# The first expert's weights and the second's gate weights loaded ahead of the last residual store

## The chip, the cores and the metric

The kernel runs on one core of a Trainium2 chip. The metric is the time of one execution on the device in microseconds. Five engines run side by side and meet through semaphores: TensorE (PE, products and transposes through the array), VectorE (DVE), ScalarE (ACT), GpSimd (POOL) and SyncE (SP), which here issues transfers. GpSimd issues transfers too. All of them are carried out by the core's 16 DMA engines.

## The reference, cut to what matters

One layer of a decoder: a token mixer (mLSTM and retention heads), then a mixture of 64 experts. There are 512 prompt tokens and 64 sample tokens, 576 in all, and D_MODEL is 1024. The change lies at the seam between the two halves:

```python
def block(x, c, pos, state, lp):
    ...
    ym, new_state = mixer(hm, pos, state, w_in, b_gates, conv_w, conv_b, m_gn, r_gn, w_out)
    x = x + gt1 * rms_norm(ym, g_mix_post)
    hf = rms_norm(x, g_ffn_pre) * (1.0 + sc2) + sh2
    B, L, D = hf.shape
    yf = moe(hf.reshape(B * L, D), w_router, b_router, w_exp_gate, w_exp_up, w_exp_down,
             w_sh_gate, w_sh_up, w_sh_down).reshape(B, L, D)
    x = x + gt2 * rms_norm(yf, g_ffn_post)

def moe(h, w_router, b_router, we_g, we_u, we_d, ws_g, ws_u, ws_d):
    s = jax.nn.sigmoid(jnp.dot(h, w_router).astype(jnp.float32))
    ...  # group-limited choice of 8 experts for each token, weights wts
    def step(acc, blk):
        e, tok, wt = blk
        xb = h[tok]
        hb = jax.nn.silu(xb @ we_g[e]) * (xb @ we_u[e])
        return acc.at[tok].add(wt[:, None] * (hb @ we_d[e]).astype(jnp.float32)), None
    ...
    shared = (jax.nn.silu(h @ ws_g) * (h @ ws_u)) @ ws_d
```

Each routed expert has gate, up and down weights of 1 MiB each (1024 x 256 in float32); the shared expert has the same sizes.

## The kernel before, in words

The tokens are cut into five tiles of 128 rows (the last has 64). Each engine has one program, whose order is the order of the code; a step waits on semaphores named in the array `S`.

**The seam.** The output product of the mixer (L1260, and L1255 for the last tile) raises `y_mm` once for each tile. ACT and VectorE normalise the rows, add them to the residual stream `x_sb` (L2049, raises `x1_done`) and make the input `hrow2` of the experts (L2060, raises `h2_ready`). For each tile SyncE stores the residual rows to HBM (`mixed_rows`, raises `st_x`) and GpSimd the rows `h` (`ffn_in_rows`, L764, raises `h2_st0` or `h2_st1`). TensorE transposes the `h` rows (`h2T_t`), makes the router's logits (L1433, L1442) and, whenever it has nothing else, steps of the shared expert's gate and up products (L1477, 64 steps, of which the trace shows two records each), spread by hand between the other operations.

**The routing.** VectorE first clears and fills small tables (L2064 to L2074). Ahead of these it waits for `ld_br` to reach 32, which stands for two loads: the router's bias (L590) and the shared expert's down weights `dn_s` (L468). Then it waits for `rl_sig`, ACT's sigmoid of the logits (L1027, L1028), chooses experts (L2086 to L2111, raises `msk_ready`), waits for the ranks of the tokens within each expert, which TensorE sums (`positions`, L1487 and L1489), and makes the first one-hot tables (`place`, L2189, raises `P_ready`). With these TensorE finds the tokens of a block (`find_idx`, L1520), VectorE writes their indices, GpSimd gathers their rows (L774), TensorE transposes them (L1533), and the expert loop begins.

**The expert loop.** Each block of 128 token slots has an up product (L1545), a transpose of the hidden rows (L1556) and a down product (L1568). The weights lie in four slots, and SyncE's one queue loads them: slots 0, 1 and 3 in `mem`, slot 2 in `x_sb`. The first three experts are fixed, all others come in the order of a sorted table (`ptab`), which raises `tab_ready`. Slot 0 and the gate half of slot 1 overlap the mixer's output weights `wo` in `mem`, which are read until the last `y_mm`; the rest of slot 1 overlaps `hrow2`; slot 2 overlaps the residual rows and needs `st_x`. GpSimd clears its gather buffers in between (L766 after `h2T_t`, L768 after `st_x`).

**SyncE's order around the change.** It stores the five residual tiles (L593), each after its `x1_done`; loads `dn_s`; waits for `h2T_t` and both `h2_st`; loads gate, up and down weights of experts 0 and 1, and gate and up of expert 2; waits for `tab_ready`; loads expert 3 and what is missing of expert 2.

Of the kernel before, what the change touches and what calls it, by code (L numbers as in the profile page):

```python
# [14 lines left out]
P = 128  # L15
D = 1024
KC = D // P
# [5 lines left out]
NT = NCH + 1  # L23
ROWS = [P] * NCH + [NS]
NCOND = 1 + NB
H = 4
# [9 lines left out]
FE = 256  # L36
# [69 lines left out]
def carve(region, at, shape, rows=P, dt=F32):  # L106

    n = 1
    for s in shape:
        n *= s  # L110
    if dt != F32:
        n //= 2
    v = region[0:rows, at:at + n]
    if dt != F32:
        v = v.bitcast(dt)
    if len(shape) == 2:
        v = v.rearrange("p (a b) -> p a b", a=shape[0])
    elif len(shape) == 3:
        v = v.rearrange("p (a b c) -> p a b c", a=shape[0], b=shape[1])
    return v, at + n  # L120
# [6 lines left out]
def build(nc, A, O, K):  # L127

    ctx = ExitStack()
    with ctx:  # L130
        def sb(name, shape, dt=F32):
            return ctx.enter_context(nc.sbuf_tensor(name, shape, dt))

        def sem(name):
            return ctx.enter_context(nc.semaphore(name))
# [4 lines left out]
        x1_d = nc.dram_tensor("mixed_rows", [T, D], F32, kind="Internal").ap()  # L140
# [3 lines left out]
        x_sb = sb("x_sb", [P, NT, D])  # L144
# [22 lines left out]
        grows, _ = carve(aux, 0, [len(GRN), T], H)  # L167
# [95 lines left out]
        adaA, _ = carve(mem, at, [2, 512])  # L263
# [18 lines left out]
        WSZ = 3 * KC * FE  # L282
# [8 lines left out]
        W_AT = [0, WSZ, None, w2_at]  # L291
# [8 lines left out]
        xg3, _ = carve(x_flat, 2 * KC * FE, [D])  # L300
# [11 lines left out]
        dn_s, at = carve(mem, at, [FJ, D])  # L312
# [44 lines left out]
        S = {n: sem(n) for n in names}  # L357
# [24 lines left out]
        for bi, (nm, _) in enumerate(BLOCKS):  # L382
            if nm in ("mv", "rv"):
                UNITS += [("tok", nm, bi, t) for t in range(NT)]
            else:
                UNITS += [("chan", nm, bi, c) for c in range(4)]
            if nm == "mv":
                UNITS += [("gate", "g", bi, 0)]
# [57 lines left out]
        def slot(r):  # L446

            return r % WSLOTS if r < NE else OVSLOTS[(r - NE) % len(OVSLOTS)]
# [5 lines left out]
        def wview(r):  # L454

            if slot(r) == XSLOT:
                return x_flat[:, 0:2 * KC * FE].rearrange("p (m c f) -> p m c f", m=2, c=KC), dnX
            w = mem[:, W_AT[slot(r)]:W_AT[slot(r)] + WSZ]
            gu = w[:, 0:2 * KC * FE].rearrange("p (m c f) -> p m c f", m=2, c=KC)
            dn = w[:, 2 * KC * FE:WSZ].rearrange("p (j d) -> p j d", j=FJ)  # L460
            return gu, dn

        def load_up(sp, w, src, s):

            sp.dma_start(w, src.rearrange("(p c) f -> p c f", c=KC)).then_inc(s, 16)

        def load_down(sp, dn, d, s):
            sp.dma_start(dn, d.rearrange("(j p) d -> p j d", p=P)).then_inc(s, 16)  # L468

        def one_expert(name, e):  # L470
            return A[name][0, bass.ds(e, 1)].rearrange("a d f -> (a d) f")
# [36 lines left out]
        def _(sp):  # L508
# [79 lines left out]
            load_up(sp, gu_s[:, 1, :, :], A["w_sh_up"][0], S["ld_ws"])  # L588
            sp.wait_ge(S["st_out"], 16 * NST)
            sp.dma_start(brow, A["b_router"][0].partition_broadcast(P)).then_inc(S["ld_br"], 16)  # L590
            for t in range(NT):
                sp.wait_ge(S["x1_done"], t + 1)
                sp.dma_start(x1_d[t * P:t * P + ROWS[t], :], x_sb[0:ROWS[t], t, :]).then_inc(S["st_x"], 16)  # L593
            load_down(sp, dn_s, A["w_sh_down"][0], S["ld_br"])
            sp.wait_ge(S["h2T_t"], NT)
            sp.wait_ge(S["h2_st0"], 16 * ((NT + 1) // 2))
            sp.wait_ge(S["h2_st1"], 16 * (NT // 2))

            def load_gate_up(r, e):
                gu, _ = wview(r)  # L600
                load_up(sp, gu[:, 0, :, :], one_expert("w_exp_gate", e), S[f"ld_gu{slot(r)}"])
                load_up(sp, gu[:, 1, :, :], one_expert("w_exp_up", e), S[f"ld_gu{slot(r)}"])

            def load_dn(r, e):
                _, dn = wview(r)
                sp.dma_start(dn, one_expert("w_exp_down", e).rearrange("(p j) d -> p j d", j=FJ)).then_inc(S[f"ld_d{slot(r)}"], 16)

            for r in range(2):
                load_gate_up(r, r)
                load_dn(r, r)  # L610
            sp.wait_ge(S["st_x"], 16 * NT)
            load_gate_up(XSLOT, XSLOT)
            sp.wait_ge(S["tab_ready"], 1)
            ids = {}
            id3 = sp.value_load(ptab[0:1, NPRE:NPRE + 1], min_val=0, max_val=NE - 1)
            load_gate_up(NPRE, id3)
            sp.wait_ge(S["gu_mm"], NSH)
            load_dn(XSLOT, XSLOT)
# [210 lines left out]
        def _(act):  # L829
# [249 lines left out]
            for i, (t, _) in enumerate(COMBINE):  # L1079
                n = ROWS[t]  # L1080
                if i < LAST:
                    act.wait_ge(S["yl_sum"], i + 1)
                    step(a(yjunk[0:n], yo[0:n, i % 2, :], ACT.Square, accum_out=stat[0:n, 10, t:t + 1]))
                    a(stat[0:n, 11, t:t + 1], stat[0:n, 10, t:t + 1], ACT.Sqrt, bias=epsc[0:n, :], scale=1.0 / D).then_inc(S["yf_rt"], 1)
                else:
                    act.wait_ge(S["yd_sum"], NT + 1)
                    step(a(yjunk[0:n, 0:512], yo[0:n, i % 2, 0:512], ACT.Square, accum_out=stat[0:n, 10, t:t + 1]))
                    step(a(stat[0:n, 13, t:t + 1], stat[0:n, 10, t:t + 1], ACT.Identity, bias=epsc[0:n, :], scale=1.0 / D))
                    act.wait_ge(S["yl_sum"], i + 1)
                    step(a(yjunk[0:n, 512:D], yo[0:n, i % 2, 512:D], ACT.Square, accum_out=stat[0:n, 0, t:t + 1]))  # L1090
                    a(stat[0:n, 11, t:t + 1], stat[0:n, 0, t:t + 1], ACT.Sqrt, bias=stat[0:n, 13, t:t + 1], scale=1.0 / D).then_inc(S["yf_rt"], 1)
# [3 lines left out]
        def _(pe):  # L1095
# [107 lines left out]
            def key_rows(h):  # L1203
                _, k = QK(h)
                for c in range(NCH):
                    tr(ps[2][:, c * P:(c + 1) * P], k[:, c * P:(c + 1) * P], ident[:, :])
# [1239 lines left out]
```

## Time and profile before

| | us |
|---|---|
| median of three timed runs | 1137.02 |
| lowest and highest | 1135.15, 1137.31 |
| span of the profiled execution | 1136.7 |
| TensorE busy in it | 1096.6 |
| VectorE, ScalarE, GpSimd busy | 462.9, 236.6, 137.3 |

The profiled execution is the same program taken by the hardware profiler; its span runs from the first to the last instruction. Operations are shown with their start and duration. A timeline merges equal operations that follow each other (x8), with the start of the first and the time until the last one ends. In square brackets stands how long the engine was idle before, and what released it. Products overlap in the array and their ends are modelled, so neighbours can overlap by some tenths of a microsecond. A stretch of the view by windows gives the busy time of each engine, the granted TensorE clock as a fraction of 2.4 GHz, the mean busy share of the DMA engines and what they moved.

### The profile page before, as it was taken

The page shows a single profiled execution, that of the slowest core. Times are in us where ns is not written, and L with a number is a line of the kernel's source. Part 1 is how long each engine was busy: PE and PEld are TensorE (multiplying, and loading weights), DVE is VectorE, ACT ScalarE, POOL GpSimd, SP SyncE. Part 2 cuts the span into 40 slices and gives each one's busy share as a digit, 9 for nine tenths or more (in the row PEclk, how much of TensorE's full clock was granted, in tenths as well). Part 3 has the DMA queues.
Part 4 walks back from the last instruction along what each step waited for, and adds up shares of the span by engine and source line. Part 5 has one row for each costly group of instructions (what it writes and reads, how often), then busy time and mean ns, then how long its engine had stood idle before and what let it go on. Part 6 is the DMA issues. An engine that isn't in the chain of part 4 may idle for free.

```text
span 1136.7 us, 16992 instructions
## 1 busy us (share of the span) xinstructions
PE 1096.6 (96%) x6443; PEld 576.4 (51%) x6443; DVE 462.9 (41%) x1286; ACT 236.6 (21%) x516; POOL 137.3 (12%) x163
## 2 busy tenths in 40 slices
PE   6999999999999999999989999999999999999896
PEld 3456677777877545754433443443343444343232
DVE  2218541665456645842264223223233232231157
ACT  4131241222233123111101111111111111111111
POOL 0110000000020110121111112111112111121100
PEclk9999999999999999999999999999999999999999
DMA  9978742042270372899999999999999999999898
GB/s 317 308 262 297 227 79 54 21 84 56 65 260 2 138 267 82 343 354 340 414 414 400 421 406 421 419 403 385 417 409 353 418 408 385 415 398 363 311 406 342
DMA packets 80743, 337.17 MB, mean 297 GB/s; under 512 B 10756, under 2 KB 27496, under 8 KB 52366
## 3 DMA queue, kind: packets, MB, share of 16 engines
q1 hardware_dynamic: 62606, 287.32, 66.4%
q0 software_dynamic: 18048, 48.68, 11.7%
q8 instruction: 54, 0.88, 0.3%
q14 instruction: 35, 0.29, 0.1%
HBM read 311.30 MB, written 37.24 MB: 307 GB/s over the span
## 4 chain that ended last, share of the span: by engine, by line
PE 87%; DMA 8%; DVE 2%; ACT 1%; issue 1%; SPq 1%; DVEq 0%; POOLq 0%; ACTq 0%
PE bank L1545 27%; PE bank L1568 15%; PE bank L1241 10%; PE bank L1260 5%; DMA mem<-in_w_exp_down 4%; PE bank L1533 3%; DMA mem<-expert_out_rows 3%; PE bank L1359 3%; PE bank L1360 3%; PE bank L1154 3%; PE bank L1477 3%; PE bank L1238 3%; PE bank L1129 1%; PE bank L1556 1%; PE bank L1324 1%
## 5 line engine op out<-in xcount | busy, mean ns | idle before, releaser
L1545 PE MATMUL bank<-mem 128*32 128x512 f32 (+2 forms) x1424 | 304.5, 594 | 2.6 <-issue 1.6
L1545 PEld LDWEIGHTS bank<-mem 128*32 128x32 f32 (+2 forms) x1424 | 100.2, 126 | 159.3 <-issue 157.9
L1568 PE MATMUL bank<-mem 128*32 128x512 f32 (+2 forms) x712 | 158.6, 599 | 5.1 <-DMA mem<-in_w_exp_down 5.1
L2231 DVE COPY mem<-bank 128x512 f32<-128x512 f32 x48 | 33.2, 692 | 292.2 <-PE bank L1533 292.2
L1545 PE MATMUL bank<-x_sb,mem 128*32 128x512 f32 (+2 forms) x480 | 141.6, 594 | 1.1 <-issue 1.1
L1241 PE MATMUL bank<-hT,mem 128*128 128x288 f32 x512 | 133.3, 409 | 1.0 <-ACT mem L919 1.0
L1241 PEld LDWEIGHTS bank<-hT,mem 128*128 128x128 f32 x512 | 93.8, 190 | 25.8 <-issue 2.4
L1049 ACT ACTIVATE mem<-bank 128x256 f32<-128x256 f32 x48 | 18.5, 385 | 316.7 <-PE bank L1556 316.5
L1568 PEld LDWEIGHTS bank<-mem 128*32 128x32 f32 (+2 forms) x712 | 49.1, 126 | 63.8 <-issue 60.3
L1568 PE MATMUL bank<-hT,mem 128*32 128x512 f32 (+2 forms) x240 | 72.8, 596 | 1.1 <-ACT mem L1049 1.1
L1545 PEld LDWEIGHTS bank<-x_sb,mem 128*32 128x32 f32 (+2 forms) x480 | 43.6, 127 | 59.1 <-issue 59.1
L2246 DVE COPY hT<-bank 128x512 f32<-128x512 f32 x48 | 33.2, 692 | 86.4 <-PE bank L1568 86.3
L774 POOL DMA_INDIRECT mem<-ffn_in_rows,idxg x32 | 33.2, 1036 | 269.8 <-DVE idxs L2227 214.4
L790 POOL DMA_INDIRECT expert_out_rows<-hT,idxs x48 | 48.8, 1017 | 115.8 <-DVE hT L2246 108.6
L1055 ACT ACTIVATE hT<-bank 128x512 f32<-128x512 f32 x48 | 28.7, 597 | 147.7 <-PE bank L1568 147.7
L1260 PE MATMUL bank<-mem 128*128 128x512 f32 x128 | 56.3, 594 | 0.0
L2189 DVE SCALAR_TENSOR_TENSOR mem<-mem,c_full 128x160 bf16<-128x160 f32 (+3 forms) x77 | 43.9, 571 | 0.3 <-issue 0.3
L1359 PE MATMUL bank<-hT,mem 128*128 128x288 f32 x128 | 42.3, 412 | 0.0
L1360 PE MATMUL bank<-hT,mem 128*128 128x288 f32 x128 | 41.5, 406 | 0.0
L1260 PEld LDWEIGHTS bank<-mem 128*128 128x128 f32 x128 | 23.8, 190 | 27.4 <-issue 27.3
L2239 DVE SCALAR_TENSOR_TENSOR mem<-mem,wtab,bank 128x128 f32<-128x128 f32 x96 | 29.4, 347 | 18.5 <-ACT mem L1043 18.5
L1037 ACT ACTIVATE mem<-bank 128x512 f32<-128x512 f32 x48 | 28.7, 598 | 39.2 <-PE bank L1533 39.2
(403 smaller groups left out, 1290.4 us busy)
## 6 DMA issues: line engine op xcount, KB each, us to landing
mem<-in_w_exp_gate SPq DMA_DIRECT2D x48, 1024.0 KB
mem<-in_w_exp_up SPq DMA_DIRECT2D x48, 1024.0 KB
mem<-in_w_exp_down SPq DMA_DIRECT2D x48, 1024.0 KB
mem<-in_w_ada SPq DMA_DIRECT2D x8, 2048.0 KB, 9.8
x_sb<-in_w_exp_gate SPq DMA_DIRECT2D x16, 1024.0 KB
x_sb<-in_w_exp_up SPq DMA_DIRECT2D x16, 1024.0 KB
hT<-in_w_exp_down SPq DMA_DIRECT2D x16, 1024.0 KB
mem<-in_w_in SPq DMA_DIRECT2D x7, 2048.0 KB, 14.2
```

Of the source, the lines that this page charges most:

```text
L790: pool.indirect_dma_start(y_d[:, :], bass.IndirectOffsetOnAxis(idxs[:, q:q + 1], 0), yo[:, q % 2, :], None, bounds_check=T * TOPK - 1, oob ...
L1154: i = mm(ps[t][:, :], hT[:, k, t * P:(t + 1) * P], ring[:, 0, k * 512:(k + 1) * 512], start=k == 0, stop=k == KC - 1)
L1238: i = mm(bank[0:n, 0:2 * DH], hT[:, k, c * P:c * P + n], w[:, k, 2 * DH * hf:2 * DH * (hf + 1)], start=k == 0, stop=k == KC - 1)
L1241: i = mm(bank[:, 0:TH], w[:, k, c * P:(c + 1) * P], hT[:, k, hf * TH:(hf + 1) * TH], start=k == 0, stop=k == KC - 1)
L1260: i = mm(y_half(t, hf), yT(k)[:, t * P:t * P + n], wo[:, k, hf * 512:(hf + 1) * 512], start=k == 0, stop=k == 2 * H - 1)
L1359: mm(A0[:, 0:TH], st, hT[:, k, 0:TH], start=k == 0, stop=k == KC - 1)
L1360: i = mm(A1[:, 0:TH], st, hT[:, k, TH:T], start=k == 0, stop=k == KC - 1)
L1477: i = mm(ps[bu if m else bg][:, 0:TH], gu_s[:, m, k, j * P:(j + 1) * P], hT[:, k, hf * TH:(hf + 1) * TH], start=k == 0, stop=k == KC - 1)
L1533: i = tr(ps[c // 4][:, (c % 4) * BLK:(c % 4 + 1) * BLK], xg[g][:, c * P:(c + 1) * P], ident[:, :])
L1545: i = mm(bank[sl, :].rearrange("p (m f) -> p m f", m=2), xT[:, j % 2, c * BLK + sl.start:c * BLK + sl.stop], wview(r)[0][:, :, c, :], star ...
L1568: i = mm(ps[4 + hf][sl, :], hhT[:, k * BLK + sl.start:k * BLK + sl.stop], wview(r)[1][:, k, hf * 512:(hf + 1) * 512], start=k == 0, stop=k ...
L2189: return stt(pm, p.to_broadcast([P, NT, w]), off, iota[:, 0:w].unsqueeze(1).to_broadcast([P, NT, w]), ALU.add, ALU.is_equal)
```

## The change

Only SyncE's program changes. After the first four residual stores it waits for the fifth `y_mm`, asks for gate, up and down weights of expert 0, then makes the fifth residual store, then asks for the gate weights of expert 1 and for `dn_s`. After the waits for `h2T_t`, `h2_st0` and `h2_st1` only the up and down weights of expert 1 are left, and expert 2 follows as before. The sizes, the addresses and the semaphores of all transfers stay.

```diff
-            for t in range(NT):
+            def load_gate(r, e):
+                load_up(sp, wview(r)[0][:, 0, :, :], one_expert("w_exp_gate", e), S[f"ld_gu{slot(r)}"])
+            def load_up_half(r, e):
+                load_up(sp, wview(r)[0][:, 1, :, :], one_expert("w_exp_up", e), S[f"ld_gu{slot(r)}"])
+            def load_gate_up(r, e):
+                load_gate(r, e)
+                load_up_half(r, e)
...
+            def x1_store(t):
                 sp.wait_ge(S["x1_done"], t + 1)
                 sp.dma_start(x1_d[t * P:t * P + ROWS[t], :], x_sb[0:ROWS[t], t, :]).then_inc(S["st_x"], 16)
+            for t in range(NT - 1):
+                x1_store(t)
+            sp.wait_ge(S["y_mm"], NT)
+            assert W_AT[0] + WSZ <= W_AT[1] and W_AT[1] + KC * FE <= 2 * H * D
+            load_gate_up(0, 0)
+            load_dn(0, 0)
+            x1_store(NT - 1)
+            load_gate(1, 1)
             load_down(sp, dn_s, A["w_sh_down"][0], S["ld_br"])
             sp.wait_ge(S["h2T_t"], NT)
             sp.wait_ge(S["h2_st0"], 16 * ((NT + 1) // 2))
             sp.wait_ge(S["h2_st1"], 16 * (NT // 2))
...
-            for r in range(2):
-                load_gate_up(r, r)
-                load_dn(r, r)
+            load_up_half(1, 1)
+            load_dn(1, 1)
             sp.wait_ge(S["st_x"], 16 * NT)
             load_gate_up(XSLOT, XSLOT)
```

SyncE's order at the seam before (`mixed_rows` are the residual stores, `in_w_sh_down` is `dn_s`, a name after "waits" is the semaphore):

```order
L593 DMA mixed_rows<-x_sb 128x1024 [waits x1_done] x4
L593 DMA mixed_rows<-x_sb 64x1024 [waits x1_done]
L468 DMA mem<-in_w_sh_down 128x2x1024
L465 DMA mem<-in_w_exp_gate 128x2048 [waits h2_st1,h2_st0,h2T_t]
L465 DMA mem<-in_w_exp_up 128x2048
L606 DMA mem<-in_w_exp_down 128x2048
L465 DMA mem<-in_w_exp_gate 128x2048
L465 DMA mem<-in_w_exp_up 128x2048
L606 DMA mem<-in_w_exp_down 128x2048
L465 DMA x_sb<-in_w_exp_gate 128x2048 [waits st_x]
```

And the same place now, where the line numbers of the later part are shifted by the new code:

```order
L608 DMA mixed_rows<-x_sb 128x1024 [waits x1_done] x4
L465 DMA mem<-in_w_exp_gate 128x2048 [waits y_mm]
L465 DMA mem<-in_w_exp_up 128x2048
L604 DMA mem<-in_w_exp_down 128x2048
L608 DMA mixed_rows<-x_sb 64x1024 [waits x1_done]
L465 DMA mem<-in_w_exp_gate 128x2048
L468 DMA mem<-in_w_sh_down 128x2x1024
L465 DMA mem<-in_w_exp_up 128x2048 [waits h2_st1,h2_st0,h2T_t]
L604 DMA mem<-in_w_exp_down 128x2048
L465 DMA x_sb<-in_w_exp_gate 128x2048 [waits st_x]
```

Three weight loads now stand ahead of the fifth residual store, and a fourth between it and `dn_s`.

On VectorE nothing moves. This is its order at the start of the routing, the same before and now but for the line numbers; `ld_br` is the semaphore of `dn_s` and of the router's bias:

```order
L2060 TENSOR_TENSOR mem<-mem 64x128x8 [waits h2_st0,h2T_t,dch]
L2064 MEMSET aux 128x120 [waits ld_br]
L2065 MEMSET aux 128x120
L2066 MEMSET mem 64x64
L2067 MEMSET mem 64x32
L2068 MEMSET mem 128x32
L2069 MEMSET mem 128x128
L2070 CAST mem<-c_full 128x128
L2071 MEMSET stat 64x1
L2072 TENSOR_SCALAR mem<-mem 128x320
L2073 TENSOR_TENSOR mem<-c_full,mem 128x320
L2074 TENSOR_SCALAR mem<-mem 128x320 [waits dch]
```

The first of these small operations waits for `dn_s`, though none of them reads it.

## Rows read from the trace of the kernel before

**Rows 1.** The page: busy us (share) by engine; shares of the chain.
```profile
PE 1096.6 (96%) x6443; PEld 576.4 (51%) x6443; DVE 462.9 (41%) x1286; ACT 236.6 (21%) x516; POOL 137.3 (12%) x163
...
PE 87%; DMA 8%; DVE 2%; ACT 1%; issue 1%; SPq 1%; DVEq 0%; POOLq 0%; ACTq 0%
```

**Rows 2.** TensorE's waits, whole span: releaser, us in total, times, longest.
```profile
PE bank L1568 <- DMA mem<-in_w_exp_down: 5.1, 3, 2.5
```

**Rows 3.** Timeline of SyncE's queue, 440 to 490: start, us, what.
```profile
444.06 9.00 SPq L593 DMA_DIRECT2D mixed_rows<-x_sb  x2
453.51 0.39 SPq L468 DMA_DIRECT2D mem<-in_w_sh_down  x1
461.23 0.33 SPq L465 DMA_DIRECT2D mem<-in_w_exp_gate  x1
...
485.98 0.35 SPq L465 DMA_DIRECT2D mem<-in_w_exp_gate  x1
```

**Rows 4.** Stretches: busy us by engine (operations), granted clock, DMA share, GB/s.
```profile
453.50:455.50 2.00, 2.00 (x18) 1.12 (x18) 0.95 (x2) 1.95 (x4) 0.00 (x0) 1.00 0.89 176
458.00:458.50 0.50, 0.48 (x7) 0.48 (x8) 0.00 (x0) 0.00 (x0) 0.24 (x1) 1.00 0.05 16
459.00:461.00 2.00, 2.00 (x11) 1.34 (x10) 1.90 (x6) 0.43 (x2) 2.00 (x2) 1.00 0.60 131
462.00:482.00 20.00, 20.00 (x98) 15.22 (x98) 17.66 (x110) 3.25 (x8) 0.11 (x1) 1.00 0.99 403
472.00:480.00 8.00, 8.00 (x42) 6.15 (x41) 7.58 (x25) 0.41 (x1) 0.00 (x0) 1.00 1.01 423
```

**Rows 5.** Timeline of VectorE, 457 to 480; brackets: idle before, releaser.
```profile
458.73 0.16 DVE L2064 MEMSET aux<- 128x120 f32 x1 [0.76 <-DMA mem<-in_w_sh_down]
...
459.42 2.20 DVE L2070 CAST mem<-c_full 128x128 bf16<-128x128 f32 x1
...
462.40 0.24 DVE L2074 TENSOR_SCALAR mem<-mem 128x320 bf16<-128x320 bf16 x1
464.11 0.49 DVE L2086 TENSOR_TENSOR aux<-mem,aux 128x320 f32<-128x320 f32 x1 [1.47 <-ACT mem L1028]
...
472.32 0.18 DVE L2111 TENSOR_SCALAR mem<-aux 64x64 bf16<-64x64 f32 x1
...
476.18 0.33 DVE L2123 CAST mem<-aux 128x320 bf16<-128x320 f32 x1
...
478.71 0.82 DVE L2189 SCALAR_TENSOR_TENSOR mem<-mem,c_full 128x640 bf16<-128x640 f32 x1
```

**Rows 6.** Timeline of TensorE's products, 439 to 490.
```profile
439.97 7.09 PE L1255 MATMUL bank<-mem 128*64 128x512 f32 x32
...
473.17 0.33 PE L1487 MATMUL bank<-mem 128*128 128x384 bf16 x1
...
479.64 0.27 PE L1520 MATMUL bank<-mem 128*128 128x7 bf16 x5
...
488.47 1.96 PE L1545 MATMUL bank<-mem 128*128 128x512 f32 x4
```

**Rows 7.** Waits of TensorE's weight loads, 470 to 490.
```profile
PEld bank L1520 <- DVE mem L2189: 0.2, 1, 0.2
```

**Rows 8.** Timeline of GpSimd, 440 to 490.
```profile
449.34 0.53 POOL L764 DMA_DIRECT2D ffn_in_rows<-mem  x1 [14.96 <-DVE mem L2060]
...
458.81 1.83 POOL L766 MEMSET mem<- 128x2048 f32 x1
460.55 0.98 POOL L768 MEMSET x_sb<- 128x1024 f32 x1
```

**Rows 9.** Stretch behind TensorE's longest stand, columns as in rows 4.
```profile
584.40:587.70 3.30, 3.30 (x5) 1.33 (x4) 3.27 (x2) 0.00 (x0) 0.20 (x1) 0.50 1.02 426
```

**Rows 10.** TensorE's products, 567 to 590: the two longest stands for weights.
```profile
568.92 3.64 PE L1568 MATMUL bank<-mem 128*32 128x512 f32 x32 [1.62 <-DMA mem<-in_w_exp_down]
...
583.48 5.40 PE L1568 MATMUL bank<-mem 128*128 128x512 f32 x8 [2.54 <-DMA mem<-in_w_exp_down]
```

More of the change, by code:

```diff
@@ L590, in _, with load_dn @@
             sp.dma_start(brow, A["b_router"][0].partition_broadcast(P)).then_inc(S["ld_br"], 16)
-            for t in range(NT):
+            def load_gate(r, e):
[5 more added lines that the diff above has]
+                load_up_half(r, e)
+            def load_dn(r, e):
+                _, dn = wview(r)
+                sp.dma_start(dn, one_expert("w_exp_down", e).rearrange("(p j) d -> p j d", j=FJ)).then_inc(S[f"ld_d{slot(r)}"], 16)
+            def x1_store(t):
                 sp.wait_ge(S["x1_done"], t + 1)
                 sp.dma_start(x1_d[t * P:t * P + ROWS[t], :], x_sb[0:ROWS[t], t, :]).then_inc(S["st_x"], 16)
+            for t in range(NT - 1):
[6 more added lines that the diff above has]
+            load_gate(1, 1)
             load_down(sp, dn_s, A["w_sh_down"][0], S["ld_br"])
@@ L597, in _ @@
             sp.wait_ge(S["h2_st1"], 16 * (NT // 2))
[L599 to L606, printed above, removed]
-            for r in range(2):
-                load_gate_up(r, r)
-                load_dn(r, r)
+            load_up_half(1, 1)
+            load_dn(1, 1)
             sp.wait_ge(S["st_x"], 16 * NT)
```

## The prediction

> **What bounds the kernel now.** I read the page first. TensorE is busy 96% of the span and holds 87% of the chain that ended last [rows 1]. So a load that arrives earlier saves time only where TensorE waits for it, and a load that arrives later costs only where TensorE ends up waiting. TensorE's list of waits over the whole span comes next [rows 2]. Expert down weights account for 5.1 us over three waits. The two longest end at 583.48 and 568.92 us [rows 10], over 100 us behind the edit. The first expert's first product (L1545) starts at 488.47 with no wait in front of it [rows 6].
>
> Are those three waits within the change's reach? Only if the transfer queues still owe work from the edit when the expert loop begins. From 461.23 on SyncE issues eight weight loads of 1 MiB, one behind the other [rows 3]. The stretch 462 to 482 moves 403 GB/s x 20 us = 8.06 MB of their 8.39 MB, and the rest needs 0.8 us at the 423 GB/s of 472 to 480 [rows 4]. So they end at about 482.8, while the next weight load is issued at 485.98, when the table of sorted experts is ready [rows 3]. The queue is empty between, and the early start of four loads can't be handed on beyond that point. The gain that the edit could have is therefore near zero: the two products it brings forward are not waited for.
>
> What it can cost lies in the stretch before. VectorE's row of operations there is dense: memsets from 458.73, the routing from 464.11, the first one-hot table of tokens (L2189) at 479.53, and TensorE's list search (L1520) behind it at 479.64 [rows 5, 6]. TensorE's weight loads show a wait of 0.2 us for exactly this L2189 [rows 7]. So the routing on VectorE sets when TensorE passes 479.6, with no slack, though TensorE looks fully busy. Whatever delays the routing delays all that follows by as much.
>
> **The change part by part.** No instruction is added on any compute engine. SyncE gets one wait (for y_mm, the last output product), and the same transfers in another order.
>
> (a) The new wait. It is met when the 32 products of L1255 end, 439.97 + 7.09 = 447.06 [rows 6]. The store queued behind it waits for x1_done of the last tile, which comes at 452.6 (before, that store's issue ends at 453.06) [rows 3]. SyncE stands idle between, so the wait itself costs nothing. Without that cover it would hold back a store by some microseconds, for which only a memset on GpSimd waits.
>
> (b) The shared expert's down weights land later. Before, that load is issued at 453.51 with only a 256 KiB store ahead of it, and VectorE stands 0.76 us in front of L2064 for it, until 458.73 [rows 3, 5]. It waits there for ld_br, the semaphore of this load, though the memsets don't touch the data. In the changed order the same SyncE queue holds, ahead of it and with it, 3 MiB + 256 KiB + 1 MiB + 1 MiB = 5.25 MiB = 5.51 MB, beginning at 447.1. At 423 GB/s [rows 4] that is 13.0 us. From issue to the start of data I take 1.7 us: 8.39 MB need 19.8 us, ended at 482.8, so began at 463.0, and were issued at 461.23. Data run from 448.8 to 461.8. GpSimd's store of 512 KiB of h rows, issued at 449.34 [rows 8], goes through the same engines and adds 0.52 MB / 423 = 1.2 us: 463.1. This is the lower end. The two transfers of 64 rows go slowly in the trace of before: 453.5 to 455.5 moved 352 KB at an engine share of 0.89, 1.0 us more than its bytes need, and 459 to 461 moved 262 KB at a share of 0.60, 1.2 us in all [rows 4]. Both added give 465.3, the upper end. Mixed with large loads they should cost less than alone, so I take 0.9 of the 2.2 us: last data at 464.0. From the end of data (458.0: the next half microsecond moves 16 GB/s [rows 4]) to L2064 it was 0.75 us; so L2064 starts at about 464.75, between 463.85 and 466.05, **6.0 us later** (5.1 to 7.3).
>
> The queue order is the crux of this term, and rows can't show it directly, since no small load stands behind large ones there. The Trainium skill (DMA: Bandwidth & Descriptors, section on queues, rings and completion order) says that each DMA engine consumes one queue's descriptors in ring order, and the section on issuing engines says that GpSimd's transfers interleave with SyncE's on the same engines. By that the down weights can't pass the four expert loads. If they could share alike with them, the landing would be near 458 and the term near zero.
>
> (c) The block of small operations gets shorter. From L2064 to the end of L2074 it took 458.73 to 462.64 = 3.91 us, of which 2.20 us is one cast of 128x128 (L2070), while a cast of 128x320 (L2123) takes 0.33 us [rows 5]. GpSimd's two memsets ran from 458.81 to 461.53, and the cast ended at 461.62 [rows 5, 8]. In the new order they still run then: the first waits for TensorE's transposes, the second for the last residual store, which lands at some 448.8 + 8.0 + 1.2 + 0.8 = 458.8 to 459.8. They are over before 464. So the cast takes 0.3 us and the block 2.0 us: **-1.9 us**. The Trainium skill (SBUF — State Buffer, the part on the two sides of SBUF) says that VectorE and GpSimd share one pair of ports, held for a whole instruction; the trace agrees with it, 2.20 us against 0.33. If the cast were long for a reason of its own, (c) would be zero.
>
> (d) The slack. VectorE then waited 1.47 us for ACT's sigmoid (L1028) before L2086 [rows 5]. ACT's chain (transposes, router, sigmoid) takes no data of these loads, so its time stays: **-1.47 us**.
>
> Sum: 6.0 - 1.9 - 1.47 = **+2.6 us**, between 5.1 - 3.4 = 1.7 and 7.3 - 3.4 = 3.9. L2086 starts at 466.7 in place of 464.11.
>
> (e) What TensorE sees of it. The mask is ready at 472.50 (L2111), TensorE's L1487 starts at 473.17 [rows 5, 6]. Later by 2.6 us: 475.1, so TensorE stands about 2.0 us there. It then works through 12 steps of shared products, and stands another 0.6 us at L1520, until VectorE's table is there at 482.1. Behind L1520 the slots table, the first gather and the sorted ids all hang on VectorE and shift alike; so does the load at 485.98. The whole loop shifts by 2.6 us.
>
> (f) The rest. The second expert's gate weights go before the down weights too (counted in (b)); its up and down weights and the third expert's gate and up weights are issued when the h rows are stored, as before. Those four MiB are through by about 476. They are needed first at 488.5, so they cost nothing; what hides them is TensorE's shared products. If this cover were gone, each MiB would cost 2.5 us. The first gather meets an empty queue either way.
>
> Against the profiled execution: 1136.7 + 2.6 = 1139.3. The median of the timed runs is 1137.02, 0.3 above that span, so I add the sum to the median: **1139.6**.
>
> **The rivals.**
> 1. *The routing is late, as summed*: 1137.02 + 1.7 to 3.9 = 1138.7 to 1140.9. Chance 0.50.
> 2. *The new stand drops TensorE's clock.* After the stand of 2.54 us before 583.48 the granted clock was 0.50 for some 3.4 us, and 8 products of L1568 took 5.40 us, while the group after the other stand took 3.64 [rows 9, 10]. After the stand of 1.62 us before 568.92 its products ran at full pace [rows 10]. The new stand of 2.0 us lies between these two, so it is open. The price is 1.8 us, of which the second stand at L1520 (0.6) takes up its part: +1.2, in all 3.8, so 1140.8 (1139.9 to 1142). Chance 0.20.
> 3. *Nothing is late enough* (not slower). The down weights land by 462.1, so that block (c) ends before ACT's sigmoid: the decisive point is 3.4 us later than before. For it speaks that the packets of four loads might share the engines with the fifth; against it, 5.5 MB need 13 us. 1136.4 to 1138.2, most likely 1137.0. Chance 0.15.
> 4. *Faster.* As in 3, and the stand at 583.48 falls under the length that drops the clock, which saves 1.8 us: 1137.0 - 1.8 = 1135.2. It would decide if the loads in front of it came 1 us earlier relative to TensorE. Against it speaks the queue that runs empty before 485.98. Chance 0.10.
> 5. *The cast keeps its 2.20 us*: 6.0 - 1.47 = 4.5, so 1141.5. Chance 0.05.
>
> **How the numbers follow.** The likeliest case is the first, so the forecast is its 1139.6. A measurement here can tell some 0.2% (2.3 us) from no change, so "slower" begins at 1139.3, close to the forecast. From case 1 about two thirds lie above it (0.33), from 2 nearly all (0.19), from 5 all (0.05): 0.57. Faster is case 4 and little else: 0.10. The rest, 0.33, is within. The range holds cases 1, 2, 5 and most of 3: 1136.8 to 1141.8.
>
> **What would show it.** Right: L2064 on VectorE waits for the down weights until about 464.7; L2070 takes 0.3 us; L2086 starts near 466.7 and no longer waits for ACT; TensorE stands about 2 us before L1487, with VectorE as the releaser, and about 0.6 us before L1520; the first L1545 starts near 491.1. Wrong: a wait for the down weights that ends before 462 (then case 3), a half clock between 474 and 480 (case 2), a long L2070 (case 5), or other waits for expert weights near 569 and 583 (case 4).

## The result, and the profile after

In the rows, line numbers of the changed kernel are 13 above those of before from the seam on (L2064 is L2077, L2086 is L2099, L1487 is L1500, L1520 is L1533, L1545 is L1558; in e3 it is 12). The changed kernel takes 1140.97 us (median of five runs, 1139.8 to 1143.8) against 1137.02 us before (five runs, 1135.15 to 1137.72). The ratio is 1.0044, with an interval from 1.0032 to 1.0055: slower by 3.6 to 6.3 us, with 5.0 us at its centre, while the medians lie 3.95 us apart. A repeat against 15 runs of the kernel before (e7 below) gives 1.0034 and 3.8 us. The forecast was 1139.6, slower by 2.6. The sign and the mechanism hold, the size does not. Among the runs told below, one of e2 (1171.93 us) and two of e4 (1427.82 and 1629.35) ran at a lower granted clock: the medians count them, the ratios don't.

In every run for which both are listed, the time of an execution is 1.8 to 1.9 us above its span. The profiled execution of after has a span of 1142.0 us and was the slowest of the five; by the same 1.8 us the profiled execution of before (1136.7) stands for 1138.5, which is 1.5 above its median. So the 5.3 us between the two profiles are not the measure of the change; what happens at one place in them is.

The page of after, engines and shares of the chain, answers to [rows 1]. TensorE's work is the same; VectorE has gone from 2% to 5% of the chain:

```profile
PE 1100.1 (96%) x6443; PEld 577.7 (51%) x6443; DVE 460.9 (40%) x1286; ACT 236.3 (21%) x516; POOL 137.0 (12%) x163
...
PE 84%; DMA 6%; DVE 5%; ACT 2%; issue 2%; SPq 0%; DVEq 0%; ACTq 0%
```

SyncE's queue, which answers to [rows 3] (start, us, operation). Gate, up and down of the first expert go at 446.71 to 448.6; the last residual store, the second gate and the shared down weights follow from 452.19; the load that waits for the sorted ids is at 489.26 in place of 485.98:

```profile
446.71 0.33 SPq L465 DMA_DIRECT2D mem<-in_w_exp_gate  x1
...
452.19 0.47 SPq L608 DMA_DIRECT2D mixed_rows<-x_sb  x1
...
454.06 0.52 SPq L468 DMA_DIRECT2D mem<-in_w_sh_down  x1
464.23 0.33 SPq L465 DMA_DIRECT2D mem<-in_w_exp_up  x1
...
489.26 0.35 SPq L465 DMA_DIRECT2D mem<-in_w_exp_gate  x1
```

VectorE, which answers to [rows 5] (in brackets the idle time before, and what ended it). The reader is to see three things. The first small operation waits 7.92 us for the shared down weights, where it was 0.76. The cast takes 0.16 us, where it was 2.20. And the first routing operation (467.41) has no bracket: the wait of 1.47 us for ACT is gone.

```profile
465.49 0.16 DVE L2077 MEMSET aux<- 128x120 f32 x1 [7.92 <-DMA mem<-in_w_sh_down]
...
466.18 0.16 DVE L2083 CAST mem<-c_full 128x128 bf16<-128x128 f32 x1
...
467.13 0.24 DVE L2087 TENSOR_SCALAR mem<-mem 128x320 bf16<-128x320 bf16 x1
467.41 0.49 DVE L2099 TENSOR_TENSOR aux<-mem,aux 128x320 f32<-128x320 f32 x1
```

GpSimd's two memsets, which answer to [rows 8], are over at 461.13, four microseconds before VectorE's small operations start:

```profile
458.41 1.83 POOL L779 MEMSET mem<- 128x2048 f32 x1
460.15 0.98 POOL L781 MEMSET x_sb<- 128x1024 f32 x1
```

TensorE, which answers to [rows 6]. It stands 2.90 us for the mask and 0.37 us for the first one-hot table; the first up product starts at 491.73. Its waits from 440 to 500, listed by total, name the same two and put both down to VectorE (the first line is the last output product of the mixer):

```profile
439.58 7.09 PE L1268 MATMUL bank<-mem 128*64 128x512 f32 x32
446.60 4.15 PE L1490 MATMUL bank<-hT,mem 128*128 128x288 f32 x16
...
475.84 0.34 PE L1500 MATMUL bank<-mem 128*128 128x384 bf16 x1 [2.90 <-DVE mem L2124]
...
482.87 0.28 PE L1533 MATMUL bank<-mem 128*128 128x7 bf16 x5 [0.37 <-DVE mem L2202]
...
491.73 7.11 PE L1558 MATMUL bank<-mem 128*128 128x512 f32 x16
```

The two executions run 0.4 us apart at this point, since TensorE's first step of shared products starts here at 446.60 and in the kernel before at 446.98:

```profile
446.98 4.15 PE L1477 MATMUL bank<-hT,mem 128*128 128x288 f32 x16
```

So I measure from this step to the first up product. It is 488.47 - 446.98 = 41.49 us before [rows 6] and 491.73 - 446.60 = 45.13 us after: **+3.64 us**, all of it in the stretch that the prediction named. From the first up product to the end of the span it is 648.2 before and 650.3 after. The experiments tell whether these other 2.1 us belong to the change.

### The profile page after: what moved, and what is told of

Its sections match the earlier page's. It is cut to its first block, busy times and chain, and to the rows that moved or that the text cites. A ratio compares the mean times of both kernels' runs of the same rounds, so it can differ in the third digit from the quotient of the medians.

```text
span 1142.0 us, 16992 instructions
## 1 busy us (share of the span) xinstructions
PE 1100.1 (96%) x6443; PEld 577.7 (51%) x6443; DVE 460.9 (40%) x1286; ACT 236.3 (21%) x516; POOL 137.0 (12%) x163
## 4 chain that ended last, share of the span: by engine, by line
PE 84%; DMA 6%; DVE 5%; ACT 2%; issue 2%; SPq 0%; DVEq 0%; ACTq 0%
PE bank L1558 27%; PE bank L1581 14%; PE bank L1254 10%; PE bank L1273 5%; DMA mem<-in_w_exp_down 4%; PE bank L1546 3%; PE bank L1372 3%; PE bank L1373 3%; PE bank L1167 3%; PE bank L1251 2%; PE bank L1672 1%; PE bank L1142 1%; PE bank L1569 1%; DMA mem<-in_w_sh_down 1%; PE bank L1337 1%
## 5 line engine op out<-in xcount | busy, mean ns | idle before, releaser
L1558 PE MATMUL bank<-mem 128*32 128x512 f32 (+2 forms) x1424 | 306.3, 595 | 2.8 <-issue 1.7
L1558 PEld LDWEIGHTS bank<-mem 128*32 128x32 f32 (+2 forms) x1424 | 101.1, 126 | 159.5 <-issue 158.1
L1558 PE MATMUL bank<-x_sb,mem 128*32 128x512 f32 (+2 forms) x480 | 143.3, 598 | 2.1 <-issue 2.1
L1558 PEld LDWEIGHTS bank<-x_sb,mem 128*32 128x32 f32 (+2 forms) x480 | 43.9, 128 | 61.4 <-issue 61.4
```

The lines of the kernel that those rows point to most:

```text
L1558: i = mm(bank[sl, :].rearrange("p (m f) -> p m f", m=2), xT[:, j % 2, c * BLK + sl.start:c * BLK + sl.stop], wview(r)[0][:, :, c, :], star ...
```

## The experiments

Each is compared with runs of the kernel before on the same chip: e1 to e4 with 31 of them, e5 to e7 with 15 on another chip. The theory: the whole loss is that VectorE waits, ahead of the routing, for a load that now stands behind four MiB in SyncE's queue. The main rival: the early weight loads cost by themselves, because they crowd the stores or disturb the loop.

**e1_own_semaphore: keep the early loads, take away what VectorE waits for.** The shared down weights raise a semaphore of their own (one that has done its earlier work by then), on which only TensorE waits, at the end of the kernel.

```diff
-            load_down(sp, dn_s, A["w_sh_down"][0], S["ld_br"])
+            load_down(sp, dn_s, A["w_sh_down"][0], S["ld_cv"])
...
-                    pe.wait_ge(S["ld_br"], 32)
+                    pe.wait_ge(S["ld_cv"], 32)
...
-            dve.wait_ge(S["ld_br"], 32)
+            dve.wait_ge(S["ld_br"], 16)
```

> The changed order of loads, but the shared expert's down weights raise a semaphore of their own, and VectorE's small operations wait for the router's bias alone. If the whole loss is the wait for those down weights: they land at about 465 as before, the small operations start near 457.6, TensorE has no stand before the ranks' product, the expert loop starts where it did before the change, and the time is 1137.0 (within 1 us). If the early weight loads themselves cost (by crowding the stores of the residual and h rows, or in the loop): 1140 to 1141, as the change.

Measured: 1136.34 us against 1137.09, ratio 0.9994 (0.9984 to 1.0004). The early loads are there: SyncE issues the first at 446.17. VectorE has its small operations behind it long before ACT's sigmoid, which is what it waits for again:

```profile
456.99 0.16 DVE L2077 MEMSET aux<- 128x120 f32 x1
...
457.68 0.23 DVE L2083 CAST mem<-c_full 128x128 bf16<-128x128 f32 x1
...
458.02 1.78 DVE L2085 TENSOR_SCALAR mem<-mem 128x320 bf16<-128x320 bf16 x1
...
463.18 0.49 DVE L2099 TENSOR_TENSOR aux<-mem,aux 128x320 f32<-128x320 f32 x1 [2.35 <-ACT mem L1041]
```

and TensorE has no stand:

```profile
446.06 4.15 PE L1490 MATMUL bank<-hT,mem 128*128 128x288 f32 x16
...
487.54 7.11 PE L1558 MATMUL bank<-mem 128*128 128x512 f32 x16
```

487.54 - 446.06 = 41.48 us, to 0.01 us the value of before. The loss is gone with the early loads in place, so crowding as a cause of the loss falls. Crowding itself is there: SyncE's wait for the stores of the h rows ends at 463.84 in e1, 3.5 us later than before on the same time scale (461.23 - 0.92), and likewise at 464.23 in the change. Here nothing on the path waits for it. Any gain falls too: with the loss taken away, four early MiB are worth nothing that can be measured (the interval leaves room for 1.8 us of gain at most).

**e2_late_down_alone: the late load without the early ones.** The kernel before, with one line moved:

```diff
-            load_down(sp, dn_s, A["w_sh_down"][0], S["ld_br"])
             sp.wait_ge(S["h2T_t"], NT)
             sp.wait_ge(S["h2_st0"], 16 * ((NT + 1) // 2))
             sp.wait_ge(S["h2_st1"], 16 * (NT // 2))
...
+            load_down(sp, dn_s, A["w_sh_down"][0], S["ld_br"])
             for r in range(2):
                 load_gate_up(r, r)
```

> The kernel before with only one edit: the shared expert's down weights are asked for behind the waits for the h rows, right ahead of the first expert's weights. No weight of an expert is loaded early. If the late landing is the whole cause: data run from 462.9 to 465.4, the small operations start at about 466.1, the first routing operation at 468.1 in place of 464.1, the loop 4.0 us later, time 1141.0. If crowding by early expert weights is the cause: 1137.0.

Measured: 1140.82 us against 1137.09, ratio 1.0032 (1.0018 to 1.0046). VectorE and TensorE:

```profile
465.11 0.16 DVE L2064 MEMSET aux<- 128x120 f32 x1 [8.35 <-DMA mem<-in_w_sh_down]
```

```profile
445.77 4.15 PE L1477 MATMUL bank<-hT,mem 128*128 128x288 f32 x16
...
475.47 0.34 PE L1487 MATMUL bank<-mem 128*128 128x384 bf16 x1 [3.35 <-DVE mem L2111]
...
491.36 7.11 PE L1545 MATMUL bank<-mem 128*128 128x512 f32 x16
```

This whole execution runs 1.21 us ahead of the kernel before at that point (445.77 against 446.98), so, moved onto the time scale of the kernel before, the small operations start at 466.3; the forecast was 466.1. The way to the first up product is 45.59 us, +4.10 against a forecast of 4.0. One moved line gives the whole loss without any early expert weight.

**e3_three_ahead: one MiB less.** The second expert's gate weights go back behind the waits:

```diff
             x1_store(NT - 1)
-            load_gate(1, 1)
             load_down(sp, dn_s, A["w_sh_down"][0], S["ld_br"])
...
-            load_up_half(1, 1)
+            load_gate_up(1, 1)
```

> The change without the second expert's early gate weights: 3 MiB in place of 4 ahead of the down weights. By the queue order one MiB is 2.5 us, so the small operations start at 463.0 in place of 465.5, the first routing operation at 464.9, which is 1.2 us late in place of 3.65; time 1138.2. If the loss doesn't follow the bytes ahead of the down weights: 1141.

Measured: 1138.48 us against 1137.09, ratio 1.0014 (1.0004 to 1.0023). VectorE:

```profile
461.44 0.16 DVE L2076 MEMSET aux<- 128x120 f32 x1 [5.17 <-DMA mem<-in_w_sh_down]
...
463.36 0.49 DVE L2098 TENSOR_TENSOR aux<-mem,aux 128x320 f32<-128x320 f32 x1
```

This execution's first shared step starts at 445.27, so the small operations start 461.44 - 445.27 = 16.17 us behind it. With four MiB (after) it is 465.49 - 446.60 = 18.89: one MiB is 2.7 us, near the 2.5 expected. Its way to the first up product is 42.41 us (487.68 - 445.27), +0.92 against the 1.2 expected. In the kernel before the same distance is 458.73 - 446.98 = 11.75, so here they are 4.42 us late. The slack (the shorter cast and the wait for ACT) takes 3.5 us of that; the rest follows the bytes ahead of the load.

**e4_down_first: the same loads, another order.** All four early expert loads are kept in front of the waits, but behind the shared down weights, so they start at 453.67, 7 us later than in the change:

```diff
-            load_gate_up(0, 0)
-            load_dn(0, 0)
             x1_store(NT - 1)
-            load_gate(1, 1)
             load_down(sp, dn_s, A["w_sh_down"][0], S["ld_br"])
+            load_gate_up(0, 0)
+            load_dn(0, 0)
+            load_gate(1, 1)
```

> The same loads as in the change, but in the order last residual store, shared down weights, then the first expert's three and the second's gate weights, all before the waits for the h rows. By the queue order the down weights land at 458.3 and the time is 1137.0. If any expert load in that stretch costs: above 1138.5.

Measured: 1137.1 us against 1137.09, ratio 1.0002 (0.9991 to 1.0012). VectorE:

```profile
458.88 0.16 DVE L2077 MEMSET aux<- 128x120 f32 x1 [1.47 <-DMA mem<-in_w_sh_down]
...
459.58 1.48 DVE L2083 CAST mem<-c_full 128x128 bf16<-128x128 f32 x1
...
463.56 0.49 DVE L2099 TENSOR_TENSOR aux<-mem,aux 128x320 f32<-128x320 f32 x1 [1.47 <-ACT mem L1041]
```

The way to the first up product is 41.48 us again (446.44 to 487.92). It is the order that costs. The loads behind the down weights are not quite without effect: the small operations start 12.44 us behind the first shared step, 0.7 us more than before, although a landing at 458.3, earlier than before, was expected. The cover takes it up.

**e5_before_own_semaphore: the same wait taken from the kernel before.** The three lines of e1, applied to the kernel before.

> The kernel before, with VectorE's wait for the shared expert's down weights taken away in the same manner (they raise a semaphore of their own). The small operations start 0.76 us earlier, but behind them VectorE waits for ACT's sigmoid anyway (1.47 us before, some 2.2 us now), so the time stays 1137.1. If that wait already cost something in the kernel before: 1136.3.

Measured: 1136.64 us against 1136.85, ratio 0.9993 (0.9983 to 1.0003), no change that can be measured. VectorE:

```profile
457.74 0.16 DVE L2064 MEMSET aux<- 128x120 f32 x1
...
458.77 2.67 DVE L2072 TENSOR_SCALAR mem<-mem 128x320 bf16<-128x320 bf16 x1
...
463.93 0.49 DVE L2086 TENSOR_TENSOR aux<-mem,aux 128x320 f32<-128x320 f32 x1 [1.81 <-ACT mem L1028]
```

It starts earlier and waits for ACT longer (1.81 us for 1.47; 2.2 were expected, but now L2072 is long, 2.67 us where it was 0.24), and the way is 41.48 us. So in the kernel before the wait of 0.76 us for the down weights cost nothing; it had 3.4 us of cover in all (1.47 of waiting and the 2 us by which the cast was longer than after the change).

**e6_down_behind_up: a larger dose.** The change, with the shared down weights one load further back, behind the waits for the h rows and the second expert's up weights:

```diff
             load_gate(1, 1)
-            load_down(sp, dn_s, A["w_sh_down"][0], S["ld_br"])
...
             load_up_half(1, 1)
+            load_down(sp, dn_s, A["w_sh_down"][0], S["ld_br"])
             load_dn(1, 1)
```

> The change with the shared down weights one step later still, behind the second expert's up weights, and so behind the waits for the h rows: issued near 464.6, data from 465.7 to 470.7, small operations at 471.4, first routing operation at 473.3 in place of 463.7. If TensorE follows VectorE one for one: loop 9.6 us late, time 1146.7. If the loop can take up some of it (its waits for weights of 5 us in all are shorter then, since the weights come early relative to TensorE): down to 1143.

Measured: 1146.38 us against 1136.85, ratio 1.0081 (1.0066 to 1.0097), that is +9.5 by the medians. VectorE and TensorE:

```profile
472.43 0.16 DVE L2077 MEMSET aux<- 128x120 f32 x1 [13.39 <-DMA mem<-in_w_sh_down]
...
474.35 0.49 DVE L2099 TENSOR_TENSOR aux<-mem,aux 128x320 f32<-128x320 f32 x1
```

```profile
482.78 0.50 PE L1500 MATMUL bank<-mem 128*128 128x384 bf16 x1 [8.39 <-DVE mem L2124]
...
483.89 8.40 PE L1490 MATMUL bank<-hT,mem 128*128 128x288 f32 x24
...
500.96 7.11 PE L1558 MATMUL bank<-mem 128*128 128x512 f32 x16
```

The first routing operation comes 474.35 - 448.05 = 26.30 us behind the first shared step, where it was 17.13 (464.11 - 446.98), so 9.2 us late (9.6 were expected, counted from 463.7 in place of the 464.11 of [rows 5]; the time forecast was 1146.7). None of it comes back in the loop, which takes 647.6 us from the first up product to the end, within the scatter of the table below. In this one execution, which was the slowest of its four (1150.48, the others 1146.1 to 1146.5), the way to the first up product is even 11.4 us longer. The stand of 8.39 us begins at 474.39. In its middle, at 478.5, TensorE's granted clock falls to 0.50, and it stays there for 10 us (a stretch with busy us by engine, granted clock, DMA share and GB/s):

```profile
478.50:488.50 10.00, 5.72 (x16) 4.08 (x17) 9.44 (x48) 0.00 (x0) 0.00 (x0) 0.50 0.04 17
```

24 records of shared products take 8.40 us there, where they take 6.07 in the profile of after. Whether the other three runs had this half clock no profile shows; their mean granted clocks, 0.989, 0.989 and 0.991, are not above the 0.991 of this one.

**e7_change_again: the change once more.**

> The change itself once more, for its spread and a second profile. The expert loop starts 3.65 us late again and the median is 1140.7 to 1141.0. Whether the half-clock stretches lie elsewhere (a second one cost 1.7 us in the first profile, near 1061) tells whether what lies beyond 3.65 us belongs to the change: if it does, the loop of this profile is again longer than before by about 2 us; if it is scatter, it is not.

Measured: 1140.62 us against 1136.85, ratio 1.0034 (1.0021 to 1.0048). VectorE and TensorE:

```profile
466.42 0.16 DVE L2077 MEMSET aux<- 128x120 f32 x1 [8.06 <-DMA mem<-in_w_sh_down]
```

```profile
447.37 4.15 PE L1490 MATMUL bank<-hT,mem 128*128 128x288 f32 x16
...
476.77 0.34 PE L1500 MATMUL bank<-mem 128*128 128x384 bf16 x1 [3.06 <-DVE mem L2124]
...
492.67 7.11 PE L1558 MATMUL bank<-mem 128*128 128x512 f32 x16
```

The way to the first up product is 45.30 us, +3.81; behind it the rest of the span is 1138.8 - 492.67 = 646.1 us, 2.1 *shorter* than before, where the first profile of the change was 2.1 longer. All in one table, from the rows above and each execution's span:

| kernel | MiB of expert weights ahead of the shared down weights | first shared step to first up product, us | from there to the end, us | time against before, us |
|---|---|---|---|---|
| before | 0 | 41.49 | 648.2 | |
| e4, down weights first | 0 | 41.48 | 646.7 | 0.0 |
| e5, before without the wait | wait gone | 41.48 | 648.9 | -0.2 |
| e1, change without the wait | wait gone | 41.48 | 648.7 | -0.8 |
| e3 | 3 | 42.41 | 649.0 | +1.4 |
| the change | 4 | 45.13 | 650.3 | +3.95 |
| the change again | 4 | 45.30 | 646.1 | +3.8 |
| e2, late without early loads | 0, but issued late | 45.59 | 647.8 | +3.7 |
| e6 | 5, and issued late | 52.91 | 647.6 | +9.5 |

The fourth column goes up and down by 4 us with no relation to the third. The 2.1 us by which it is longer in the first profile of the change do not come back in the second, so they are scatter between executions; what makes it, these profiles do not settle.

## Why the prediction was right and where it was wrong

**The bound, and no gain: right.** TensorE was named as the bound with no wait for the first expert's weights, and the queue as empty before the sorted ids. After the change the eight loads are through by 476 (476 to 478 moves 16 GB/s), the next one is issued at 489.26, and e1 and e4 show that early loads alone give nothing.

**(a) The new wait costs nothing: right.** The 32 products of the last output tile end at 439.58 + 7.09 = 446.67, the first weight load goes at 446.71, and the store behind the wait still goes at 452.19, which is 452.57 on the time scale of before, where its issue ended at 453.06 [rows 3].

**(b) The landing of the shared down weights: the right mechanism, too small a size, and the step that failed.** The term was put at 6.0 us and measured 7.1 to 7.3. I put L2064 at 464.75, within 463.85 to 466.05. On the time scale of before it came at 465.49 + 0.38 = 465.87 in the first profile and at 466.42 - 0.39 = 466.03 in the second: at the upper end. Here are the stretches of the profile of after, columns as in [rows 4]:

```profile
447.00:449.00 2.00, 2.00 (x10) 1.58 (x9) 1.66 (x2) 1.37 (x5) 0.05 (x1) 1.00 0.53 156
449.00:451.00 2.00, 2.00 (x12) 1.58 (x11) 1.86 (x5) 0.01 (x1) 0.48 (x1) 1.00 1.02 401
451.00:454.00 3.00, 3.00 (x20) 2.15 (x20) 1.56 (x2) 2.32 (x5) 0.00 (x0) 1.00 0.99 333
454.00:463.50 9.50, 9.03 (x73) 6.24 (x70) 3.38 (x3) 3.26 (x10) 3.26 (x3) 1.00 1.01 420
463.50:464.00 0.50, 0.50 (x3) 0.39 (x3) 0.00 (x0) 0.48 (x3) 0.00 (x0) 1.00 0.75 303
464.00:464.50 0.50, 0.50 (x3) 0.38 (x2) 0.00 (x0) 0.50 (x1) 0.00 (x0) 1.00 0.27 107
464.50:465.00 0.50, 0.50 (x3) 0.38 (x2) 0.00 (x0) 0.49 (x2) 0.00 (x0) 1.00 0.06 25
```

And the kernel before, just ahead of the half microsecond of [rows 4] that moves 16 GB/s:

```profile
457.50:458.00 0.50, 0.05 (x2) 0.00 (x0) 0.47 (x1) 0.38 (x1) 0.00 (x0) 1.00 0.91 369
```

The start of data was right to 0.2 us: the 312 KB moved by 449.0 put it at 448.26, or 448.6 on the time scale of before, where I had 448.8. The stretches from 447 to 465 move 6.3 MB. SyncE's 5.51 MB and both of GpSimd's stores (0.52 + 0.26 MB) make 6.29 MB, so both stores had passed by the time the load landed; in the sum I had counted the first store in full and only 0.9 us for everything else. At 423 GB/s the 0.26 MB alone are 0.6 us, and the 3 us from 451 to 454 ran at 333 GB/s, which is another 0.6 us: 1.2 where I had taken 0.9. Why those 3 us were slow no row shows: SyncE's 64-row store, which I had blamed for such a loss, was issued at 452.19 behind three MiB, and by the queue of each packet less than 0.1 MB of GpSimd's first store falls in them.

The larger part is the tail. The queue runs at 420 GB/s until 463.5 and then fades over 1.5 us, at 303, 107 and 25 GB/s. Before, with one MiB in the queue, traffic went from 369 to 16 GB/s within half a microsecond, and I took the 0.75 us from there to L2064 as the whole price of a landing. From the end of the full rate to L2077 it is now 2.0 us; in the second profile of the change (full rate until 464.5, L2077 at 466.42) and in e3 (459.5, 461.44) it is 1.9. At 423 GB/s the 0.22 MB of the fade would have been through at 464.0, 1.5 us ahead of L2077 for the 0.75 that I had. So of the miss of 1.1 us some 0.7 is the tail and some 0.4 the bytes and their rate. Of the cause of the tail no more than this is known: the packets of the trace, taken by queue, put GpSimd's second store between 461.5 and 463.5, and the bytes of the fade are SyncE's. That the 16 DMA engines finish at different times behind a long queue is my inference from the fading, and no row by engine shows it.

The Trainium skill (DMA: Bandwidth & Descriptors, on queues, rings and completion order) has one queue's descriptors consumed in ring order on each engine. The runs agree: 0 MiB, 3 MiB and 4 MiB ahead put the first small operation 12.4 us (e4: 458.88 - 446.44), 16.2 and 18.9 us behind the first shared step. By the sharing that the third rival supposed the three would lie close together.

**(c) The shortened cast: right.** 2.20 us became 0.16, the block 3.91 became 1.88 (465.49 to 467.37). In six more profiles the cast takes 0.16 or 0.23 us and starts outside GpSimd's memsets; in e4 it starts at 459.58 amid them and takes 1.48 us. That it is the overlap and not the cast is shown by e1 and e5, where VectorE comes earlier: there the cast is short (0.23 us), and the next large operation, a TENSOR_SCALAR of 0.24 us elsewhere, starts amid the memsets and takes 1.78 and 2.67 us; it ends at 459.80 and 461.44, each 0.1 us behind the end of a memset. No run moved the memsets alone. The Trainium skill (SBUF — State Buffer, on the two separate sides of SBUF) has VectorE and GpSimd share one pair of ports, which the one that starts first holds for its whole instruction; the traces agree with it.

**(d) The slack: right.** The 1.47 us are gone, and e3 shows that they and the shorter cast were slack: 4.42 us late at the first small operation, 0.92 at the first up product.

So the sum by its terms is 7.15 - 2.03 - 1.47 = 3.65, and the way to the first up product grew by 3.64. The forecast terms were 6.0 - 1.9 - 1.47 = 2.6. So 1.15 of the miss is in (b), and 0.13 that (c) gained more than forecast hides a little of it.

**(e) What TensorE sees: right in form.** 2.0 and 0.6 us of standing were forecast, 2.90 and 0.37 measured. The first follows the delay (0.16 us in e3, 3.06 in e7, 3.35 in e2); the second is 0.37 or 0.38 in all of them, whatever the first is.

**The forecast of the time.** 1137.02 + 3.65 = 1140.7; two medians of the change, 1140.97 and 1140.62, lie on both sides of it. The measured time lay 0.1 us above case 1's range of 1138.7 to 1140.9, and within the whole range. The sum stood at 2.6 us because (b) was taken near the middle of its bounds, and (b) came out at the upper one.

**Rival 2, the clock:** it did not happen in either profile of the change. TensorE stood 2.90 and 3.06 us before the ranks' product and the clock stayed at full rate. In e2 it stood 3.35 us, with the same outcome. At this place only the 8.39 us of e6 brought a half clock. **Rival 3** (nothing is late enough) and **rival 5** (the cast stays long) are refuted by the rows. **Rival 4** (faster) too: with the loss taken away in e1, the interval of the ratio includes 1. The sign that the prediction named for it, other waits near 569 and 583, did appear (1.98 and 0.84 us where they were 1.62 and 2.54), but e5, whose loads are those of the kernel before, has 1.41 and 2.71 there, and the second profile of the change only one, of 1.93: these waits differ from one execution to the next, and the sign tells nothing.

## What to carry to other kernels

A queue that carries transfers in order is a schedule: putting something early in it puts everything behind it late, and the thing to look up is not who waits for the load that is moved but who waits for the ones it overtakes, down to the small and apparently unimportant. Here the one who waited didn't even need the data: a semaphore shared by the small load of the router's bias and a large one that is needed 600 us later (L1659, at 1076 us in the kernel before) made the second a condition of the first. Give loads with different consumers different semaphores; and price a landing behind a long queue by all bytes of all queues plus a tail (here 2 us from the end of the full rate, with four or five MiB queued), not by the quick landing of a lone load.

## What the runs showed of the hardware

TensorE's clock does not follow the length of a stand alone, as my second rival had it. In the kernel before, the stand of 2.54 us before 583.48 was followed by the half clock [rows 9, 10]. Here is the same group of eight products in four other runs:

```profile
580.25 3.70 PE L1581 MATMUL bank<-mem 128*128 128x512 f32 x8 [2.62 <-DMA mem<-in_w_exp_down]
584.43 3.70 PE L1568 MATMUL bank<-mem 128*128 128x512 f32 x8 [2.68 <-DMA mem<-in_w_exp_down]
582.52 5.40 PE L1580 MATMUL bank<-mem 128*128 128x512 f32 x8 [2.71 <-DMA mem<-in_w_exp_down]
579.50 5.40 PE L1581 MATMUL bank<-mem 128*128 128x512 f32 x8 [1.86 <-DMA mem<-in_w_exp_down]
```

They are from e1, e2, e3 and e4. At full clock (1.00 granted) the group takes 3.70 us, at half clock (0.50) 5.40. Stands of 2.62 and 2.68 us brought no half clock, one of 1.86 us did. Stands of 2.90, 3.06 and 3.35 us before the ranks' product brought none either, while in the profile of after one of 1.98 us did (granted clock 0.50 from 573.3 to 576.5), and one of 2.12 us before 1061.27 too:

```profile
572.20 5.34 PE L1581 MATMUL bank<-mem 128*32 128x512 f32 x32 [1.98 <-DMA mem<-in_w_exp_down]
```

TensorE's waits for down weights in that profile, which answer to [rows 2], are shorter than before (3.7 us in all over three waits), and the time is longer all the same.

Where such a stretch falls differs from one execution to the next of the same kernel: it is near 573, 1061 and 1082 in the first profile of the change and near 585 and 1080 in the second. One costs some 1.7 us (5.40 - 3.70; the prediction's 1.8 set 5.40 against a group of another shape). The Trainium skill (TensorE: Matmul & The Clock Gate, part 1) says that the monitor behind the clock runs free and isn't aligned with the kernel; by that rule, the same stand may or may not bring the half clock, and the traces agree.

The half clock is not the whole scatter. From the first up product to the end, e2 has none before its last microseconds and takes 647.8 us; the second profile of the change has two and takes 646.1. So two single profiles of this kernel can't be subtracted to better than a few microseconds, while the way between two steps in the same profile repeats to 0.2 us.
